# Sixteen more tokens on the gathered side of an expert layer, and neuron matmuls of 368 columns

## The reference

```python
def peer(h, w_query, sub_keys, u_emb, v_emb):
    t = h.reshape(B * N, D)                                      # 512 tokens
    q = (t @ w_query).reshape(T, PEER_HEADS, 2, PEER_HALF)       # 8 heads
    s = jnp.einsum('thpk,pnk->thpn', q, sub_keys).astype(jnp.float32)
    s_val, s_idx = lax.top_k(s, PEER_TOPK)                       # 16 of 128, for each half
    ...                                                          # 16 best pairs: expert, gate (T, 8, 16)
        act = jax.nn.gelu(jnp.einsum('td,ted->te', tb, ub), approximate=False) * gb
        return jnp.einsum('te,ted->td', act, vb)
```

## Time and profile before

| | |
|---|---|
| median of three runs | 3464.65 us (3460.77 to 3469.7) |
| profiled execution | 3466.85 us, of which the span of the profile is 3465.0 us |
| TensorE busy | 3378.7 us (98%) |
| VectorE, ACT, POOL busy | 2155.6, 1186.4, 1829.8 us |
| DMA | 874.71 MB, 252 GB/s over the span |
| neuron units | about 1258 to 2386 us |
| sweep units | about 2386 to 3452 us |

### The profile page before, as it was taken

How to read it: one execution, slowest core, us unless ns; L and a number is a source line. 1 busy time by engine, 2 the same in 40 slices (tenths; PEclk the granted TensorE clock), 3 DMA queues, 4 the chain that set the end, 5 groups by cost and what they waited for, 6 DMA issues and landing times.

```text
span 3465.0 us, 44031 instructions
## 1 busy us (share of the span) xinstructions
PE 3378.7 (98%) x16931; PEld 2932.8 (85%) x16931; DVE 2155.6 (62%) x3280; ACT 1186.4 (34%) x1632; POOL 1829.8 (53%) x904
## 2 busy tenths in 40 slices
PE   6999999999999999999999999999999999999998
PEld 3688888766888899999999999998887888888887
DVE  2288887746414759993766676644655566556656
ACT  3322221234223232223555556533232232222223
POOL 1210000213444355676666666666877777777775
PEclk8999999999999999999999999999999999999999
DMA  9655643565423236776677777788888878878872
GB/s 380 245 191 202 217 163 115 176 229 204 172 97 146 86 141 234 265 295 267 265 302 300 311 270 284 313 314 332 339 309 317 335 290 342 332 281 313 340 278 108
DMA packets 184618, 874.71 MB, mean 252 GB/s; under 512 B 16621, under 2 KB 77501, under 8 KB 97844
## 3 DMA queue, kind: packets, MB, share of 16 engines
q1 hardware_dynamic: 122160, 525.38, 41.1%
q0 software_dynamic: 38688, 281.15, 20.4%
q10 hardware_dynamic: 23652, 66.69, 5.1%
HBM read 803.78 MB, written 69.32 MB: 252 GB/s over the span
## 4 chain that ended last, share of the span: by engine, by line
PE 85%; DVE 7%; DMA 3%; POOL 2%; issue 1%; ACT 1%; ACTq 0%; SPq 0%; DVEq 0%; POOLq 0%
PE bank L2120 80%; PE bank L2381 2%; DMA ring<-in_w_mod 2%; PE bank L2498 1%; POOL split L807 1%; DMA ring<-in_v_emb 1%; PE bank L2355 1%; DVE b L1880 1%; POOL low L765 1%; DVE rows_a L1819 1%; PE bank L2128 1%; DVE b L1860 0%; DVE rows_c L1819 0%; PE bank L2481 0%; DVE tiny L1875 0%
## 5 line engine op out<-in xcount | busy, mean ns | idle before, releaser
L807 POOL TENSOR_TENSOR split<-ring,split 128x1024 fp32r<-128x1024 f32 x544 | 1343.2, 2481 | 569.4 <-ACT split L1145 567.2
L2120 PE MATMUL bank<-h_hi,split 128*128 128x384 f32 (+1 forms) x4608 | 1221.8, 341 | 8.2 <-POOL split L807 6.9
L2120 PE MATMUL bank<-split,a_split 128*128 128x512 f32 x4608 | 1051.4, 390 | 15.2 <-POOL split L807 15.0
L1145 ACT ACTIVATE split<-ring 128x1024 fp32r<-128x1024 f32 x544 | 574.0, 1060 | 1437.2 <-PE bank L2120 1257.9
L2120 PEld LDWEIGHTS bank<-split,a_split 128*128 128x128 f32 x4608 | 864.5, 188 | 201.8 <-POOL split L807 18.5
L2120 PEld LDWEIGHTS bank<-h_hi,split 128*128 128x128 f32 x4608 | 839.7, 188 | 29.6 <-POOL split L807 8.8
L2120 PE MATMUL bank<-h_lo,split 128*128 128x384 f32 (+1 forms) x2304 | 785.6, 341 | 0.0
L2120 PEld LDWEIGHTS bank<-h_lo,split 128*128 128x128 f32 x2304 | 433.5, 188 | 9.5
L1995 DVE TENSOR_TENSOR acc<-acc,bank 128x512 f32<-128x512 f32 x180 | 121.9, 682 | 331.0 <-PE bank L2120 331.0
L2120 PE MATMUL bank<-hT_hi,w_hi 128*128 128x512 f32 (+1 forms) x768 | 289.3, 377 | 5.3 <-POOL ring_lo L727 2.2
L2120 PE MATMUL bank<-hT_lo,w_hi 128*128 128x512 f32 (+1 forms) x768 | 287.2, 374 | 0.0
(11 more groups left out here) (318 smaller groups left out, 3846.0 us busy)
## 6 DMA issues: line engine op xcount, KB each, us to landing
ring<-in_u_emb SPq DMA_DIRECT2D x128, 1024.0 KB, 4.8
ring<-in_v_emb SPq DMA_DIRECT2D x128, 1024.0 KB, 10.4
ring<-in_w_mod SPq DMA_DIRECT2D x48, 1024.0 KB, 8.2
ring<-in_w_in SPq DMA_DIRECT2D x44, 1024.0 KB, 5.9
ring<-in_w_mod SPq DMA_DIRECT2D x64, 512.0 KB, 4.7
neurons<-tiny ACTq DMA_DIRECT2D x128, 192.0 KB
gate_table<-b ACTq DMA_DIRECT2D x6, 4096.0 KB, 15.0
weigh<-neurons SPq DMA_DIRECT2D x32, 768.0 KB
```

The lines of the kernel that those rows point to most:

```text
L807: nc.gpsimd.tensor_tensor(split[:, r % 2, 1, at].bitcast(F32R), ring[:, r % 4, :, :].rearrange("p k n -> p (k n)")[:, at], split[:, r % 2, ...
L1145: nc.scalar.activation(split[:, q % 2, 0, at].bitcast(F32R), ring[:, q, :, :].rearrange("p k n -> p (k n)")[:, at], ACT.Copy)\
L2120: last = mm(out_, left[a].bitcast(F32R), right[b].bitcast(F32R), start=start and n == 0, stop=stop and n == 2)
```

## The change

The last 16 dense tokens (EXTRA = 16) move to the gathered side. Each of these 16 tokens is laid out eight times over the partitions, and partition group g (16 partitions) takes the token's slots 16 g to 16 g + 15. So 16 more gathers of 128 rows serve all 128 slots of the 16 tokens. A neuron matmul has TN = 368 columns. To be able to cut there, `h2_hi` and `h2_lo` are laid out in groups of 16 tokens (group, k-tile, token) instead of tiles of 128. The stored neurons of the 16 tokens are zeros, so that the sweep adds nothing for them; its matmuls stay as they are.

The `h2` rows of these tokens go through DRAM (`extra_dram`) and come back as row SLOTS of the gather sequence; ACT copies it over the 128 gathered tokens' rows when these are done. The indices and gates are moved into the layout by 16 small DMAs, one in each of the neuron units 44 to 59. In the sweep 16 rows of `v` are weighted and added up in the four PSUM banks, ACT copies the sum out, and in pass E_PASS = 3 four matmuls with a selection matrix `sel` (which adds the eight groups) add it to the third tile's sums.

The rows are scheduled by a list, `ROW_UNIT`, the unit in which VectorE uses row n. Rows 0 to 112 keep their units (3 to 115). Then two rows a unit for 116 to 125, four for 126, and two for each of the sweep units 0 to 3; the 16 extra rows of `v` from sweep unit 6 to 18, and the 128 rows of `v` from 18 to 116, none at k = 7. A `u` row is gathered one unit ahead of its use, as before; a `v` row now right after the split of the unit that uses it. ACT's sweep loop is written out.

```diff
+EXTRA = 16
+EG = P // EXTRA
+TN = TD - EXTRA
+U_ROWS = SLOTS + 1 + EXTRA
+ALL_ROWS = U_ROWS + EXTRA + SLOTS
...
+def row_units():
+
+    at = list(range(3, 3 + PRE - 3))
+    for unit in range(PRE, NK - 2):
+        twice = unit >= PRE + CHUNKS * CHUNK_UNITS or (EXTRA > 16 and unit % 8 == 0)
+        at += [unit] * (2 if twice else 1)
+    at = at[:U_ROWS - 4] + [NK - 2] * 4 if len(at) > U_ROWS - 4 else at + [NK - 2] * 4
+    unit = NK
+    while len(at) < U_ROWS:
+        if unit % 8 != 7:
+            at += [unit] * min(2, U_ROWS - len(at))
+        unit += 1
+    units = [u for u in range(unit + 2, 2 * NK - 11) if u % 8 != 7]
+    first = (len(units) * EXTRA + (EXTRA + SLOTS) // 2) // (EXTRA + SLOTS)
+    later = len(units) - first
+    return at + [units[m * first // EXTRA] for m in range(EXTRA)] +         [units[first + m * later // SLOTS] for m in range(SLOTS)]
+
+
+ROW_UNIT = row_units()
+E_ACT = ROW_UNIT[U_ROWS - 1] - NK + 1
+E_COPY = ROW_UNIT[U_ROWS + EXTRA - 1] - NK
+E_PASS = E_COPY // 8 + 1
...
-            h2_hi = region("h2_hi", 8192, search)[:, :].rearrange("p (j k t) -> p k j t", j=LT, t=P)
+            h2_hi = region("h2_hi", 8192, search)[:, :].rearrange("p (g k t) -> p k g t", k=KT, t=EXTRA)
...
+        gate_e, nval_e, nval_last_e = (soft[:, i * EXTRA:(i + 1) * EXTRA] for i in range(3))
+        gate_part, idx_part = mask[wide, 0, :], mask[wide, 1, :].bitcast(U32)
+        sel = mask[:, 0, :]
+        sum_e = x2_dense[:, JD - 1, :]
...
+                if n == SLOTS:
+                    pool.wait_ge(e_moved, 16 * 3 * EG)
...
-                pool.indirect_dma_start(gathered_rows[n % 3], None, u_rows[:, :] if n < SLOTS else v_rows[:, :],
-                                        bass.IndirectOffsetOnAxis(row_idx[:, n % SLOTS:n % SLOTS + 1], 0))\
-                    .then_inc(gathered[n % 3], 16)
+                if n == SLOTS:
+                    pool.dma_start(gathered_rows[n % 3], extra_dram[:, :]).then_inc(gathered[n % 3], 16)
+                    return
+                if n < SLOTS:
+                    which = row_idx[:, n:n + 1]
+                elif n < U_ROWS + EXTRA:
+                    m = n - SLOTS - 1 if n < U_ROWS else n - U_ROWS
+                    which = idx_e[:, m:m + 1]
+                else:
+                    m = n - U_ROWS - EXTRA
+                    which = row_idx[:, m:m + 1]
+                pool.indirect_dma_start(gathered_rows[n % 3], None, u_rows[:, :] if n < U_ROWS else v_rows[:, :],
+                                        bass.IndirectOffsetOnAxis(which, 0)).then_inc(gathered[n % 3], 16)
 
             for r in range(1, V0 + NK):
                 rest_half(r, 0)
                 rest_half(r, 1)
-                if 0 <= r - (U0 + 2) < SLOTS:
-                    gather_rows(r - (U0 + 2))
-                for m in range(SLOTS):
-                    if V0 + 2 + m - m // 8 == r:
-                        gather_rows(SLOTS + m)
+                for n in range(ALL_ROWS):
+                    if U0 + ROW_UNIT[n] - (n < U_ROWS) == r:
+                        gather_rows(n)
...
+                if r == 4:
+                    act.wait_ge(h2_made, 2)
+                    for g in range(EG):
+                        act.dma_start(extra_dram[g * EXTRA:(g + 1) * EXTRA, :], sh2_row[extra, :]).then_inc(e_moved, 16)
...
-                nc.scalar.activation(neuron_out[:, q % 2, :], bank[:, 4 + q % 2, 0:TD], ACT.Gelu)\
+                nc.scalar.activation(neuron_out[:, q % 2, 0:TN], bank[:, 4 + q % 2, 0:TN], ACT.Gelu)\
                     .then_inc(gelu_made, 1)
...
+                if unit == PRE:
+                    act.wait_ge(idx_made, 6)
+                if unit < PRE + 2 * EG:
+                    g = (unit - PRE) // 2
+                    part, rows = (idx_part, idx_e) if unit % 2 == 0 else (gate_part, gate_e)
+                    act.dma_start(rows[g * EXTRA:(g + 1) * EXTRA, :], part[32 - EXTRA:32, g * EXTRA:(g + 1) * EXTRA])\
+                       .then_inc(e_moved, 16)
...
+                if k == ROW_UNIT[SLOTS]:
+                    rows = gathered_rows[SLOTS % 3]
+                    act.wait_ge(gathered[SLOTS % 3], 16 * (SLOTS // 3 + 1))
+                    act.wait_ge(rows_used, SLOTS)
+                    nc.scalar.activation(bank_rows[:, 0:D - P], rows[:, 0:D - P], ACT.Copy)
+                    nc.scalar.activation(h2_last, rows[:, D - P:D], ACT.Copy).then_inc(rows_used, 1)
...
+                if unit == E_ACT:
+                    act.wait_ge(nval_summed, 2)
+                    nc.scalar.activation(nval_e, nval_e, ACT.Gelu).then_inc(nval_gelu, 1)
...
+                if unit == E_COPY:
+                    act.wait_ge(rows_used, U_ROWS + EXTRA)
+                    nc.scalar.activation(sum_e, bank_rows, ACT.Copy).then_inc(e_copied, 1)
+                if unit == 8 * E_PASS + 8:
+                    act.wait_ge(split_used, 2 * (V0 + 8 * E_PASS + 7) + 2)
+                    act.dma_start(x2_dense[:, JD - 1, :], x2_dram[TD - P:TD, :]).then_inc(last_rows, 16)
...
+                if k == 8:
+                    nc.vector.scalar_tensor_tensor(sc2_row[wide, :], x2[wide, JD - 1, :], rstd2[wide, JD - 1:JD],
+                                                   sc2_row[wide, :], ALU.mult, ALU.mult).then_inc(a2_made, 1)
+                if k == 10:
+                    dve.wait_ge(a2_made, 9)
+                    nc.vector.tensor_tensor(sh2_row[wide, :], sc2_row[wide, :], sh2_row[wide, :], ALU.add)\
+                        .then_inc(h2_made, 1)
...
+            dve.wait_ge(e_moved, 16 * EG)
...
+            dve.wait_ge(soft_on_dve, 2)
+            nc.vector.tensor_copy(gate_part, gate[wide, JD - 1, :, :].rearrange("p h k -> p (h k)")).then_inc(idx_made, 1)
...
-            def add_rows(m):
-
-                n = SLOTS + m
+            def add_rows(n):
+
+                weight = act_s[:, n - U_ROWS - EXTRA:n - U_ROWS - EXTRA + 1] if n >= U_ROWS + EXTRA else \
+                    nval_e[:, n - U_ROWS:n - U_ROWS + 1]
                 dve.wait_ge(gathered[n % 3], 16 * (n // 3 + 1))
                 rows = gathered_rows[n % 3].rearrange("p (b n) -> p b n", b=4)
-                if m == 0:
-                    nc.vector.tensor_scalar(sparse_bank, rows, act_s[:, 0:1], None, ALU.mult).then_inc(rows_used, 1)
+                if n in (U_ROWS, U_ROWS + EXTRA):
+                    if n > U_ROWS:
+                        dve.wait_ge(e_copied, 1)
+                    nc.vector.tensor_scalar(sparse_bank, rows, weight, None, ALU.mult).then_inc(rows_used, 1)
                     return
                 dve.wait_ge(rows_used, n)
-                nc.vector.scalar_tensor_tensor(sparse_bank, rows, act_s[:, m:m + 1], sparse_bank, ALU.mult, ALU.add)\
+                nc.vector.scalar_tensor_tensor(sparse_bank, rows, weight, sparse_bank, ALU.mult, ALU.add)\
                     .then_inc(rows_used, 1)
...
             weigh_group(0)
-            dot(NK - 5)
+            dot(ROW_UNIT.index(NK - 2))
+            dot(ROW_UNIT.index(NK - 2) + 1)
             rest_group(0)
             weigh_group(1)
-            dot(NK - 4)
             rest_group(1)
-            rows_added = 0
+            dot(ROW_UNIT.index(NK - 2) + 2)
+            dot(ROW_UNIT.index(NK - 2) + 3)
...
+                if unit == E_ACT:
+                    dve.wait_ge(rows_used, U_ROWS)
+                    dve.wait_ge(e_moved, 16 * 3 * EG)
+                    nc.vector.tensor_tensor(nval_e, nval_e, nval_last_e, ALU.add).then_inc(nval_summed, 1)
+                    nc.vector.memset(sel[:, 0:P - EXTRA], 0.0)
+                    nc.vector.tensor_reduce(sel[:, extra], ident.rearrange("p (g t) -> p t g", t=EXTRA), AX.X, ALU.add)
...
-                        last = mm3(bank[:, 4 + q % 2, 0:TD].rearrange("p (j t) -> p j t", t=P),
+                        last = mm3(bank[:, 4 + q % 2, 0:TN].rearrange("p (g t) -> p g t", t=EXTRA),
                                    [split[:, q % 2, w, k * P:(k + 1) * P] for w in range(2)],
-                                   [h2_hi[:, k, 0:JD, :], h2_lo[:, k, 0:JD, :]], k == 0, k == KT - 1)
+                                   [h2_hi[:, k, 0:TN // EXTRA, :], h2_lo[:, k, 0:TN // EXTRA, :]], k == 0, k == KT - 1)
                     last.then_inc(split_used, 1)
...
+                    if extra_rows and s and j == JD - 1:
+                        at = k // 2 * NB
+                        mm(bank[:, 4 + o % 4, :], sel, sum_e[:, at:at + NB], start=False, stop=False)
...
-            with pe.Fori(1, GROUPS // 2) as i:
+            with pe.Fori(1, E_PASS) as i:
+                for k in range(8):
+                    sums(i, k)
+            pe.wait_ge(e_copied, 1)
+            for k in range(8):
+                sums(E_PASS, k, False, True)
```

72 lines of the change are left out of this document (46 added, 26 removed).

## The result

The changed kernel takes 3506.0 us (median of four runs, 3500.45 to 3513.99) against 3465.29 us for the kernel before (3460.77 to 3469.7): a ratio of 1.0112, 95% interval 1.0087 to 1.0137. It is slower by 1.1%, and 61 us above the forecast.

What follows compares the result with a forecast made beforehand. TensorE, busy 98% of the span, was taken as the bound. Narrower matmul -33.3, denser gathers +18, sweep -8 and extra sums +3.5 gave -19.8 us: 3445 us, range 3416 to 3477.

Steps and rivals of the forecast that it cites:

- The narrower matmul: Neuron stage: 368 columns take 166.7 ns instead of 173.3, 0.32 us a unit, 41.0 us over 128 units; short runs cost 0.
- the upper bound: Moving-operand reads in neuron and query matmuls: each run start costs at most one 2.4 GHz clock, 0.417 ns.
- Rival 3: Neuron and query matmuls: each short run start costs TensorE a clock, 0.417 ns; 3498 us, chance 0.10.
- The line of N columns: TensorE matmuls: start-to-start time grows 0.417 ns a column, one column per 2.4 GHz clock, so 368 columns take 166.7 ns.
- rival 4: Neuron stage: weight loads set the pace and the matmul stays at 173.3 ns; 3478 us, chance 0.04.
- Where the gain can't be had: First 24 neuron units: VectorE's search sets PE's pace, so they give back nothing; 104 units leave 33.3 us.
- The seam: Denser gathers from the neuron stage's end into the first sweep units: +18 us, 14 for bytes and 4 for one stop.
- the -33.3: Neuron stage: the narrower matmul's gain, 0.32 us in each of 104 units.
- its upper bound of 30: Denser gathers before the sweep: at most +30 us, since waits chain up there.
- the stops: Before the sweep: neuron stores behind the table store, row 128, and POOL's gather awaiting a product; 4 us for one.
- The sweep: Later v gathers remove GpSimd's row-buffer wait at pass seams: -8 us, bounds -16.6 and +12.
- +3.5 us: Sweep pass 3: four extra fp32 sum matmuls of 512 columns, 0.87 us each, all on PE's path.

Runs made afterwards that it cites:

- Experiment 1: Kernel before, its 384-column neuron matmuls reading the moving side in runs of 16, 32, 64 or 384 words (wrong words): 3478.86 us, single run.
- packed, spread: Changed kernel with h2's dense words copied by ACT into one run per neuron matmul, u rows spread, third x2 load later: 3438.92 us, ratio 0.9928.
- one-run: Changed kernel with neuron matmuls and query blocks 1 to 3 reading one run each (wrong words): 3476.54 us, ratio 1.0031.
- after: The changed kernel itself, against the kernel before: 3506.0 us, ratio 1.0112.
- packed: Changed kernel with h2's dense words copied by ACT so query and neuron matmuls read one run, gather schedule untouched (also spelled pack_after): 3473.36 us, ratio 1.0032.
- Experiment 4: Changed kernel with 15 dense u rows moved to units 44 to 115 and unit 126's last two gathered later (the spread kernel): 3471.14 us, ratio 1.0015.
- experiment 5: Kernel before with only the v rows gathered later, right after the split of the sweep unit using them: 3459.64 us, ratio 0.998.
- experiment 7: Changed kernel with u rows spread as in Experiment 4, plus the third tile's x2 load four sweep units later: 3469.63 us, ratio 1.0012.
- pack_spread0: The packed, spread kernel without the later gathers of unit 126's last two rows: 3441.86 us, ratio 0.9922.

## Why the prediction was wrong

**The narrower matmul: the step that failed.** The prediction read that one run and four runs take the same time and wrote "three more run starts cost nothing to within a nanosecond; I take 0 for twenty more". The runs it compared were of 128 and 512 words, and the change has runs of 16. Experiment 1 shows that runs of 64 words and more are free and those of 32 and 16 are not: 9.1 / 23 = 0.40 ns for each further run start at 16 words, 4.3 / 11 = 0.39 at 32. The number of starts was not the whole question, their length was, and no row of the trace had a short one. By experiment 1's price the 22 more starts of a 368-column matmul are 8.8 ns against 6.7 won: 175.5 ns, and 173.3 to 174.8 was measured. In the query 31 starts by 0.40 are 12.4 ns; the stage grew by 11.3 us / 768 = 14.7 ns a matmul, and with one run it is back at 195.9 us. So the price of a start is no constant: 0.30 to 0.37 ns in the neurons, 0.47 in the query, which is over the 0.417 that the prediction called the upper bound; no row stood behind that bound. Rival 3 had this mechanism and asked for more than 0.33 ns a start; it put the time at 3498 us, the nearest of all, and it had a chance of 0.10. That it came so near is partly luck: it added 52.6 us for the matmuls, where about 46 were missed, and nothing for the seam and the sweep, where 13 were. What spoke against it was an extrapolation from 128 words to 16.

The Trainium skill ("Advanced Engine Details and Errata", Memory Cachelines) gives SBUF lines of 16 bytes, and beside rival 3 the prediction drew from it that runs of 64 bytes lose nothing. Experiment 1 disagrees: runs of 64 and of 128 bytes do lose, and those of 256 don't.

**The line of N columns.** One column per 2.4 GHz clock held: 368 columns in one run take 166.7 ns (units of 8.00 us). Some units take 8.11 instead, a second rhythm of the same matmuls, so the stage of units 44 to 115 gained 16.8 us and not 72 x 0.32 = 23.0. What sets the rhythm was not found. The weight loads do not set the pace, rival 4 was wrong.

**Where the gain can't be had.** Right for units 0 to 23: 211.6 to 213.6 us in every kernel. But the bound reaches further than unit 24. In packed, spread, units 24 to 43 take 167.9 us against 169.1; 20 x 0.32 = 6.4 us were to be had, and the waits for GpSimd's splits there, 6.9 us (3.7 in one-run), show what took them.

**The seam: right mechanism, wrong size.** +18 us was taken, of which 3.8 only cancel the gain that the -33.3 has for units 116 to 127: net 14.2. Against before the seam grew by 24.4 + 4.9 = 29.3 us, 15.1 more. Of these 5.6 belong to the short runs (the seam is 182.8 us in after, 177.2 in packed) and 9.5 to the seam itself. Experiment 4 gives 182.8 - 149.4 = 33.4 back, 4.1 more than the growth, since sweep units 3 and 4 take 8.2 and 8.7 us in it instead of 11.3 and 9.8 before. In the prediction's gross terms the seam cost 29.3 + 3.8 = 33.1 us, beyond its upper bound of 30, and 27.5 without the short runs. Each of the stops was named (the store's queue, row 128, the products behind which POOL stands) and they were taken one at a time: 10 us for the bytes, with the 3.8, and 4 for one stop. By the timelines they came together: a late row makes the product late (VectorE's 6.49 us), that the gather (POOL's 7.91), and that the split (PE's 5.32); and one stop behind four gathers in a row was 10.36 us, not 4 to 6. The restart at 1.2 GHz adds (307 - 174) x 9 = 1.2 us to it.

**The sweep.** POOL's waits for VectorE went, as forecast. -8 us was taken; alone it is worth 5.4 us (experiment 5), and in the changed kernel the sweep from unit 6 on is 0.7 us shorter with the four extra sums in it. These, +3.5 us by the prediction, are units 25, 27, 29 and 31, each 0.88 us longer: right. Not foreseen was that the x2 load in unit 32 makes `v_emb` late by 17.8 us, units 35 and 36 being 14.5 and 9.6 us long; with the load later (experiment 7) both are back at 8.2 to 8.3 us in the spread kernel.

**The sum of what was measured.** Forecast -33.3 + 18 - 8 + 3.5. Measured, by stage: -0.2 for the neurons up to unit 116, +11.3 for the query, +29.3 for the seam, -0.7 for the rest of the sweep with the sums in it, -3.1 ahead of the query: 36.6 (36.5 in the span). The miss of 56 us splits as follows. The short runs made 34.4, by after against packed: 11.2 in the query, -2.0, 1.1 and 18.5 in the neurons up to unit 116, 5.6 in the seam. Gains that would not have come in any case are 11.6: 5.4 up to unit 44, for VectorE's and GpSimd's pace, and 6.2 up to unit 116, for the second rhythm. The seam itself made 9.5 and the sweep 3.8; the 3.1 ahead of the query, which the change didn't make, go off.

## What to carry to other kernels

When a layout is cut finer so that an edge can be placed freely, price the access pattern by a run of the length that it will have; a pattern with few long runs says nothing of one with many short ones. If two uses want different widths of the same operand, a repacking by an idle engine between them can be nearly free (here 30 copies of 0.5 us cost TensorE 0.75 us) where both compromises, short runs and a cut matmul, cost 1%. And extra gathers belong where the DMA share is 0.75, not where it is 1: the same rows cost 23.5 us at the seam (pack_after against pack_spread0) and nothing that a stage shows in units 44 to 115 (628.3 us in both).

## What the runs showed of the hardware

A matmul of 384 columns starts 173.3 ns after the last if its fp32 moving operand lies in runs of 64 words or more, 177.6 ns in runs of 32 and 182.4 in runs of 16 (with the output written in as many groups); a stride of 240 words between runs of 16 gives 177.3, strides of 32 to 128 give 180.7 to 182.0. With one run, start to start is (N + 32) / 2.4 GHz for 512, 384, 368 and 256 columns (226.7, 173.3, 166.7, and 118 to 120 ns); in other stretches of the same kernels those of 368 columns are 169.0 ns apart (8.11 us a unit). The Trainium skill ("TensorE: Matmul & The Clock Gate", Back-to-back issue gap) gives N / 2.4 plus 2.5 ns for a matmul by itself; the slope agrees and the constant here is 13.3 ns, for fp32 with a weight load before every matmul. For a stream of such pairs the same section gives about 131 ns at N = 512; this case measured 226.7 ns, for fp32. A matmul of 144 columns does not follow either line: paired with one of 368 it took 280 ns together, where (368 + 32 + 144 + 32) / 2.4 would be 240.
